# A two-layer mixer trunk on one core: the first dilated pair's probabilities turned by transposes and DMAs instead of on TensorE

## What is computed

```
s = einsum(q, gathered k) * scale; s = where(valid, s, -inf)   # for windows (128,1), (512,4), (2048,16)
p = softmax(concat of the three, axis=-1)
out = sum over the windows of einsum(p_c, gathered v_c)
y_d = dilated(dq, dk, d_v) * silu(g_d)
x = x + concat([y_a, y_b, y_c, y_d]) @ w_out
```

## Time and profile before

| what | value |
|---|---|
| median of 3 runs | 807.24 us (807.17 to 807.83) |
| the profiled execution's own time | 806.72 us |
| its span | 804.9 us |
| PE busy | 796.2 us (99%) |
| DVE, ACT, POOL busy | 608.1, 469.2, 127.5 us |
| TensorE clock granted, all 40 slices | 9 tenths or more |
| DMA engines busy, by slice | 4 to 9 tenths |
| PE's idle time by cause, all lines together | 5.0 us, of it 1.3 us before L921 |

### The profile page before, as it was taken

The page is one execution under the profiler, slowest core; times in us unless marked ns, Lnnn a source line. Parts: engine busy times, 40 slices in busy tenths (PEclk is TensorE's granted clock), DMA queues, the critical chain, the costliest instruction groups (busy, mean ns, idle before and its releaser), DMA issues.

```text
span 804.9 us, 10724 instructions
## 1 busy us (share of the span) xinstructions
PE 796.2 (99%) x3900; PEld 674.0 (84%) x3900; DVE 608.1 (76%) x1066; ACT 469.2 (58%) x762; POOL 127.5 (16%) x199
## 2 busy tenths in 40 slices
PE   8999999999999999999999999999999999999998
PEld 5888888999887888888888888889998888888886
DVE  6678889787899776665764967988779987865552
ACT  6666543857955676443556465447777566664431
POOL 7100000020432421102100000002105242211000
PEclk9999999999999999999999999999999999999999
DMA  8966534575698987869866655365767988968563
GB/s 332 344 219 215 182 132 152 160 252 187 211 283 262 288 256 243 261 208 280 259 213 187 194 152 196 111 188 170 228 200 238 268 277 256 274 196 286 187 195 115
DMA packets 54117, 178.22 MB, mean 221 GB/s; under 512 B 7408, under 2 KB 8352, under 8 KB 54064
## 3 DMA queue, kind: packets, MB, share of 16 engines
q1 hardware_dynamic: 44736, 149.98, 57.2%
q0 software_dynamic: 9008, 27.34, 12.3%
q10 hardware_dynamic: 320, 0.21, 0.1%
HBM read 161.76 MB, written 15.75 MB: 221 GB/s over the span
## 4 chain that ended last, share of the span: by engine, by line
PE 78%; DVE 12%; issue 3%; ACT 3%; DMA 3%; POOL 0%; SPq 0%; DVEq 0%; ACTq 0%; POOLq 0%
PE gemm L764 24%; PE gemm L755 24%; PE gemm L756 23%; DVE w_lo L1434 4%; DVE arena L1395 3%; DMA raw<-in_weights_dram 1%; DMA arena<-dil_q_squares 1%; PE pairs L921 1%; ACT w_hi L1051 1%; DVE u L1694 1%; PE pairs L811 1%; DVE arena L1523 1%; ACT arena L1231 1%; DMA mla_P_squares<-u 1%; PE pairs L946 0%
## 5 line engine op out<-in xcount | busy, mean ns | idle before, releaser
L1434 DVE TENSOR_TENSOR w_lo<-raw,w_hi 128x1024 fp32r<-128x1024 f32 (+2 forms) x279 | 322.1, 1163 | 151.8 <-ACT w_hi L1051 150.7
L755 PE MATMUL gemm<-w_hi,a_hi 128*128 128x512 f32 (+2 forms) x1080 | 414.5, 384 | 0.7 <-ACT w_hi L1051 0.7
L756 PE MATMUL gemm<-w_hi,a_lo 128*128 128x512 f32 (+2 forms) x1080 | 408.9, 379 | 0.0
L1051 ACT ACTIVATE w_hi<-raw 128x1024 fp32r<-128x1024 f32 (+2 forms) x279 | 278.2, 1011 | 212.7 <-PE gemm L764 138.6
L764 PE MATMUL gemm<-w_lo,a_hi 128*128 128x512 f32 (+2 forms) x1080 | 278.2, 379 | 0.3
L755 PEld LDWEIGHTS gemm<-w_hi,a_hi 128*128 128x128 f32 x1080 | 202.9, 188 | 37.3 <-issue 1.7
L756 PEld LDWEIGHTS gemm<-w_hi,a_lo 128*128 128x128 f32 x1080 | 202.9, 188 | 33.5
L764 PEld LDWEIGHTS gemm<-w_lo,a_hi 128*128 128x128 f32 x1080 | 199.5, 188 | 36.4 <-DVE w_lo L1434 1.9
L637 POOL TENSOR_TENSOR st<-st,powers 128x4 f32<-128x4 f32 (+2 forms) x8 | 3.7, 461 | 296.6 <-ACT arena L1129 213.0
L1081 ACT ACTIVATE u<-gemm,st 128x512 f32<-128x512 f32 (+2 forms) x36 | 21.3, 644 | 14.6 <-PE gemm L764 14.6
L1395 DVE STREAM_TRANSPOSE arena<-u 32x256 f32<-32x256 f32 x64 | 27.9, 436 | 1.2
(11 more groups left out here) (218 smaller groups left out, 672.8 us busy)
## 6 DMA issues: line engine op xcount, KB each, us to landing
raw<-in_weights_dram SPq DMA_DIRECT2D x225, 512.0 KB, 4.3
raw<-in_weights_dram SPq DMA_DIRECT2D x38, 384.0 KB, 3.6
raw<-in_weights_dram SPq DMA_DIRECT2D x16, 344.0 KB, 3.3
y_squares<-arena POOLq DMA_DIRECT2D x8, 512.0 KB, 3.4
arena<-y_squares POOLq DMA_DIRECT2D x32, 128.0 KB, 5.5
x<-in_x_dram SPq DMA_DIRECT2D x4, 512.0 KB, 6.2
o<-ssd_rows SPq DMA_DIRECT2D x8, 256.0 KB, 5.3
param_rows<-in_params_dram SPq DMA_DIRECT2D x2, 904.0 KB, 6.6
```

The source lines that it names most:

```text
L755: pe.matmul(acc_t[t], a_hi[:, k, tok[t]], hi, start=k == 0, stop=False)
L756: pe.matmul(acc_t[t], a_lo[:, k, tok[t]], hi, start=False, stop=False)
L1051: A_(w_hi[:, g % SPLIT, 0:c], raw[:, g % RAW, 0:c], ACT.Copy).then_inc(hi_done, 1)
L1434: TT(w_lo[:, g % SPLIT, 0:c], raw[:, g % RAW, 0:c], w_hi[:, g % SPLIT, 0:c].bitcast(F32), ALU.subtract).then_inc(split_done, 1)
```

## The change

The probabilities of the first dilated pair go by squares too. Six PE transposes per layer (`dil PT 0`) fall away with their PSUM pair; DVE gets two stream transposes (`dil P 0 squares`, slot 102, directly behind the taps); POOL gets one DMA out and four back; ACT's `dil PT 0` now copies from `u` in place of PSUM, at slot 107. The tile that is written and read back is the one that mla P 0 used, in `u`. The second pair stays on PE. On PE `dil O 0` moves from slot 104 to 106, `dil PT 1` from 106 to 107, `dil O 1` from 108 to 109. DVE's scores of pair 1 wait for the new squares where they waited for the PE transposes. POOL's order at the end of a layer becomes dil P 0, y 0, y 1, y 2, and dil P 0's way out takes over the place behind the wait for mla P 1.

```diff
-          "dil PT 0": 102, "dil S 1": 103, "dil O 0": 104, "dil PT 1": 106, "dil O 1": 108}
+          "dil S 1": 103, "dil O 0": 106, "dil PT 1": 107, "dil O 1": 109}
...
-LAST_READER |= {f"dil PT {_i}": ("act", f"dil PT {_i}") for _i in range(2)}
+LAST_READER["dil PT 1"] = "act", "dil PT 1"
...
+        SQUARES["dil P 0"] = SQUARES["mla P 0"]
...
-                for name in ("y 1", "y 0", "y 2"):
+                for name in ("dil P 0", "y 0", "y 1", "y 2"):
                     squares_out(l, name)
                     squares_back(l, name)
...
-                    if m == "mla":
-                        act_.wait_ge(squares_in[f"mla P {i}"], 16 * 4 * (l + 1))
-                        if i:
-                            act_.wait_ge(*pe("mla O 0"))
+                    if (m, i) != ("dil", 1):
+                        act_.wait_ge(squares_in[f"{m} P {i}"], 16 * 4 * (l + 1))
+                        if (m, i) != ("mla", 0):
+                            act_.wait_ge(*pe("mla O 0" if i else "mla O 1"))
...
-                                if n == (slot(f"dil PT {i}") if m == "dil" else slot(f"mla O {i}", 1)):
+                                if n == (slot("dil PT 1") if (m, i) == ("dil", 1) else slot(f"{m} O {i}", 1)):
                                     probs_T(m, i)
...
                     if m == "dil":
-                        v.wait_ge(*(pe("dil PT 0") if i else me("mla P 1 squares")))
+                        v.wait_ge(*me("dil P 0 squares" if i else "mla P 1 squares"))
...
                                     if m == "dil":
                                         taps(i)
+                                        if not i:
+                                            probs_squares("dil", 0)
```

More of the change, by code:

```diff
@@ L250 @@
         "mla cT, ssd Y, mla rT, "
-        "mla S 0, mla S 1, mla O 0, dil S 0, mla O 1, dil PT 0, dil S 1, dil O 0, "
+        "mla S 0, mla S 1, mla O 0, dil S 0, mla O 1, dil S 1, dil O 0, "
         "dil PT 1, dil O 1",
     "act":
-        "x rs sum, evac 0, evac 1, gla lr, gla abs, gla exp, gla ln, evac 2, gla E 0, gla E 1, "
-        "gla E 2, gla cross, gla E 3, gla E 4, evac 3, gla E 5, gla E 6, gla E 7, evac 4, ssd abs, ssd exp, "
-        "ssd eA, ssd ln, conv 3 1, gla rs sum, conv 3 0, evac 5, ssd silu 1, "
@@ L257 @@
-        "mla crs sum, ssd gcol, ssd silu 0, evac 6, ssd exp 0, mla cT, ssd xD, ssd exp 1, mla q 0, evac 7, mla q 1, mla rs 0 sum, "
[3 rows of a table removed]
-    "dve":
[L262 to L268, removed]
[3 rows of a table removed]
+        "x rs sum, evac 0, evac 1, gla lr, gla abs, gla exp, gla ln, evac 2, gla E 0, gla E 1, gla E 2, gla cross, gla E 3, "
@@ new lines @@
+        "gla E 4, evac 3, gla E 5, gla E 6, gla E 7, evac 4, ssd abs, ssd exp, ssd eA, ssd ln, conv 3 1, gla rs sum, conv 3 0, "
+        "evac 5, ssd silu 1, mla crs sum, ssd gcol, ssd silu 0, evac 6, ssd exp 0, mla cT, ssd xD, ssd exp 1, mla q 0, evac 7, "
+        "mla q 1, mla rs 0 sum, mla kv 0, mla kv 1, mla rs 1 sum, dil rs 0 sum, evac 8, dil rs 1 sum, mla qT, evac 9, mla rT, "
+        "mla P 0, ssd rs sum, mla P 1, evac 10, mla PT 0, dil q, dil P 0, mla PT 1, evac 11, dil P 1, dil PT 0, yT 0, dil PT 1, "
@@ new lines @@
+        "yT 1, yT 2, evac 12, yT 3",
+    "dve":
+        "pad, gla turn, gla dots, gla zero 0, gla zero 1, gla la, gla scan 0, gla scan 1, gla D 0, gla D 1, gla W 0, gla D 2, "
+        "gla W 1, gla D 3, gla W 2, gla merge 1, gla D 4, gla W 3, gla merge 2, gla D 5, gla W 4, gla merge 3, gla D 6, gla W 5, "
+        "gla merge 4, gla D 7, gla W 6, gla merge 5, gla W 7, gla merge 6, ssd turn, gla merge 7, ssd dt0, ssd dt, ssd la, "
+        "conv 1 0, conv 1 1, gla o, conv 1 2, conv 1 3, conv 1 4, conv 1 5, ssd row, conv 0 0, conv 0 1, conv 0 2, conv 0 3, "
+        "conv 0 4, conv 0 5, ssd CB, mla cn, ssd x squares, ssd E 0, mla cT, ssd E 1, ssd M 0, ssd xdt, ssd M 1, mla n 0 0, "
+        "mla n 0 1, ssd yT, mla q squares, mla n 1 0, ssd y squares, mla n 1 1, mla rope products, mla rope, mla k squares, "
+        "dil n 0 0, dil n 0 1, dil n 1 0, dil n 1 1, dil rope 0 products, dil rope 0, dil rope 1 products, dil rope 1, gated 1, "
+        "mla max 0, mla nmax 0, dil q squares, dil k squares, mla P 0 squares, mla max 1, mla nmax 1, y 1, mla P 1 squares, "
[3 rows of a table added]
@@ L1264, in probs_T @@
                 def probs_T(m, i):
-                    if m == "mla":
-                        act_.wait_ge(squares_in[f"mla P {i}"], 16 * 4 * (l + 1))
-                        if i:
-                            act_.wait_ge(*pe("mla O 0"))
-                        to, squares = PT.rearrange("p r (c i a) -> p i (r c) a", i=4, a=32), SQUARES[f"mla P {i}"][1].rearrange("p (i x a) -> p i x a", i=4, a=32)
-                        A_(to, squares, ACT.Copy).then_inc(*signal("act", f"mla PT {i}"))
+                    if (m, i) != ("dil", 1):
+                        act_.wait_ge(squares_in[f"{m} P {i}"], 16 * 4 * (l + 1))
+                        if (m, i) != ("mla", 0):
+                            act_.wait_ge(*pe("mla O 0" if i else "mla O 1"))
+                        to, squares = PT.rearrange("p r (c i a) -> p i (r c) a", i=4, a=32), SQUARES[f"{m} P {i}"][1].rearrange("p (i x a) -> p i x a", i=4, a=32)
+                        A_(to, squares, ACT.Copy).then_inc(*signal("act", f"{m} PT {i}"))
                         return
@@ L1741, in taps, with probs_squares @@
                     last.then_inc(*sig(f"dil P {i}"))
-                def probs_squares(i):
-                    v.wait_ge(*act(f"mla P {i}"))
-                    if not i:
+                def probs_squares(m, i):
+                    v.wait_ge(*(act if m == "mla" else me)(f"{m} P {i}"))
+                    if (m, i) == ("mla", 0):
                         v.wait_ge(*me("dil k squares"))
-                    to = SQUARES[f"mla P {i}"][0].rearrange("p (f r c a) -> p r f c a", f=4, r=2, c=3)
+                    to = SQUARES[f"{m} P {i}"][0].rearrange("p (f r c a) -> p r f c a", f=4, r=2, c=3)
                     for r in range(2):
                         last = v.transpose(to[:, r], Pb[:, r].rearrange("p (c f b) -> p f c b", c=3, f=4))
-                    last.then_inc(*sig(f"mla P {i} squares"))
+                    last.then_inc(*sig(f"{m} P {i} squares"))
                 def out_heads(m, i):
@@ L1900, in _ @@
                             if n == SQUARES[f"mla P {i}"][2]:
-                                probs_squares(i)
+                                probs_squares("mla", i)
                         for j in Y_TURN:
```

## The result

The changed kernel takes 824.3 us (median of 4 runs, 823.2 to 827.4) where the kernel before takes 807.2: a ratio of 1.0214, 95% interval 1.0189 to 1.0238. Slower, as forecast, but by 17 us instead of 7.6, and beyond the upper end of the range, 820.0. The profiled execution took 823.24 us, its span 821.3: 16.4 more than before.

The account below looks back on a forecast made before the run. PE, busy 796.2 of 804.9 us, was taken to set the time. Removed transposes -1.36 and stalls +2.4 and +6.6 gave +7.6 us, so 814.8 us forecast, range 808.0 to 820.0.

Parts of the forecast that it names:

- The mechanism: POOL's extra trip lands y 2 late; behind yT 2 on ACT, evac 12 and hi make PE stall at slot 115.
- What is added on POOL: One more round trip ahead of y 0, y 1, y 2 in POOL's serial queue; yT 2 5.2 and 9.0 us late.
- The moves of O 0, PT 1 and O 1 on PE by one or two slots change no sum: PE's moved jobs around slots 104 to 109 were costed at nothing.
- The bounds: Extra trip costs the chain 5.8 to 10.4 us, second layer 5.7 to 12.1; total +2.0 to +13.0, 809.2 to 820.2 us.
- The argument that ACT's wait frees the engines: ACT waiting at yT 1 pauses SP's weight loads, so y 2's out was taken as 6.1 us, 7.0 in second layer.
- The sum: -1.36 us for transposes removed, +2.4 and +6.6 us for PE's stalls at slot 115: +7.6 us.
- What is removed: Six PE transposes per layer, 0.68 us each block, 1.36 us for both layers, all gained on PE.
- The new copy is late: Rival: PE waits at dil O 0 for dil P 0's copy, 0.2 us or 2 us more per layer; 815 to 818; chance 0.03.
- Every leg contended, 820 us: Rival: all POOL legs run at contended prices, giving the upper bound, 820 us; chance 0.06.
- The gain alone: Rival: every POOL leg takes its free price, no stall, PE keeps the 1.36 us; 805.9 us; chance 0.17.

Follow-up runs that it names:

- run 3: Kernel before plus DVE's squares and an unread round trip of dil P 0, placed last, behind y 2 on POOL; 806.87 us, ratio 0.998.
- run 4: Changed kernel with only POOL's order altered: each way out issued ahead of the way back before it; 807.3 us, ratio 0.9993.
- run 9: Changed kernel with POOL issuing y 1's and y 0's outs before its wait for mla P 1's squares, then dil P 0's out, then backs; 807.95 us, ratio 0.9993.
- Run 8: Changed kernel with evac 12 put ahead of yT 2 on ACT; 810.87 us, ratio 1.0029.
- run 7: Changed kernel with y 1 ahead of y 0 on POOL, behind dil P 0; 822.41 us, ratio 1.0149.
- run 10: Kernel before plus two unread round trips of dil P 0, one after the other, ahead of y 1, y 0, y 2; no slot moved; 831.27 us, ratio 1.0282.
- run 2: Kernel before plus DVE's squares and one unread round trip of dil P 0 ahead of y 1, y 0, y 2; 811.39 us, ratio 1.0043.
- run 1: Kernel before with only the changed kernel's moved slots and orders; all transposes on PE, no extra trip; 808.22 us, ratio 0.999.
- run 5: Changed kernel, unedited, on a second chip; 823.07 us, ratio 1.0168 to the kernel before there.
- run 6: Kernel before with the moved slots and an unread round trip ahead of y 0, y 1, y 2; PE keeps its transposes; 820.5 us, ratio 1.0116.
- run 11: Changed kernel with the early outs of run 9 and evac 12 ahead of yT 2 on ACT; 807.2 us, ratio 0.9986.

## Why the prediction was right in its mechanism and wrong in its size

**The mechanism held.** Runs 3, 4 and 9 leave all the work in place and only move it in POOL's queue: the loss disappears. Run 8 leaves y 2 late and takes evac 12 out of the way: most of it disappears. So in the changed kernel the serial chain, the late y 2, and evac 12 and hi behind yT 2 are the cause, in the order in which the prediction has them. (Runs 7 and 10 have a loss of the same kind by another result: there y 0 is late, and ACT's wait at yT 0 is what PE pays.) The rows that it named are there: four trips on POOL, L1070 waiting for `y_squares`, the first load of slot 115 released by ACT's w_hi, PE with 12 matmuls fewer. Their sizes are not: ACT waits 6.4 and 4.2 us at yT 2 where 5 and 9 were named, 6.1 and 8.5 at yT 1 where 4 was, 4.2 and 5.0 at yT 0 where nothing was, and PE is busy for longer, not shorter.

The forecast sum was +7.6 and the spans differ by 16.4. The 8.8 between them are three terms: the stalls 12.74 for 9.0 (+3.7), the clock 3.99 for nothing (+4.0), the gain -0.33 for -1.36 (+1.0).

**"What is added on POOL", the value for y 1's out: the step that failed.** It was taken as 4.6 and 4.8 us, "the place that y 2's out had". Measured 7.63 and 7.73. That row was read as if a leg's price belonged to its place in time. It belongs to what else runs beside it, and the change had altered that. In the kernels whose slots are not moved the out issued at 301 to 304 us, and its fellow in the second layer, takes what the prediction says: 3.7 and 4.8 (before), 4.9 and 4.2 (run 2), 5.3 and 4.5 (run 3). With the moved slots it takes 6.4 and 8.8 (run 1, with no trip at all), 7.6 and 7.7 (after), 7.5 and 7.6 (run 5), 7.7 and 6.8 (run 6), 8.4 and 8.0 (run 7, so the order of y 0 and y 1 isn't it), 6.8 and 8.0 (run 8). The sentence "The moves of O 0, PT 1 and O 1 on PE by one or two slots change no sum" is right for PE's own work and wrong for this leg. What differs is the traffic: in the row that was read the loads paused. The DMA queues while y 2's out was pending before, and while y 1's was in the changed kernel, first layer (packets, MB, share):

```profile
q0 software_dynamic: 231, 0.73, 66.9%
q1 hardware_dynamic: 68, 0.28, 28.9%
```

```profile
q0 software_dynamic: 312, 0.96, 45.0%
q1 hardware_dynamic: 327, 1.22, 44.9%
```

0.28 MB of weights (q1) in 3.66 us against 1.22 in 7.63. The legs behind a back line up by it: 3.76 us with no weights at all in run 7, 3.92 and 3.79 in run 10; 4.81 with 0.72 MB (before, second layer); 6.4 with 1.12 (run 1); 7.63 and 7.73 with 1.22 and 1.42 (after). Others do not fit: y 2's outs in run 2, 5.58 with 0.05 MB and 8.82 with 0.43, and in after, 7.67 and 9.71 with 1.05 each. A long leg also gives the loads more time, so the amounts prove no rate; but the legs near 3.8 stand behind a back and are hardly longer than the 3.6 of an out in a free queue, so standing there costs little by itself.

By step, first layer: the new out 0.8 us later than taken, its leg 4.0 for 3.6, y 0's 6.75 for 7.9, y 1's 7.63 for 4.6, y 2's 7.67 for 6.1. Together y 2's back is 4.5 us later than forecast (318.3 for 313.8), its landing somewhat faster, and the stall 5.8 for 2.4. Second layer: 5.0 for 3.6, 6.7 for 9.4, 7.7 for 4.8, 9.7 for 7.0, that is 3.8 later, but y 2 was at ACT 4.7 us after its back was issued, where 7.85 were taken. The stalls, 6.9 for 6.6, agree only because two errors cancel, and 2.0 of them lie ahead of slot 115, at a hi and a lo that yT 1's wait of 8.5 us had delayed; the prediction had no wait there.

The bounds failed with the same step. They added one trip of 5.8 to 10.4 us to a chain whose other legs stayed as they were, so that yT 2 would be at most 7.5 us late in the first layer; it was 9.0 late. In the second it was 9.8 late, within its 5.7 to 12.1.

**The argument that ACT's wait frees the engines** was right and put in the wrong place. The prediction used it for y 2's leg alone. It was not strong enough there: ACT waited 6 us at yT 1, and 1.05 MB of weights moved all the same. Where ACT waits 14 and 13 us, as in run 7, y 2's out does drop to 3.8 in both layers; where it waits 9, as in run 2, it takes 5.6 and 8.8. In the changed kernel y 0 comes first, yT 0 waits only 4.2 and 5.0 us, and the loads go on.

The Trainium skill, DMA: Bandwidth & Descriptors, "Anatomy of one DMA — SWDGE (gpsimd) path", gives by its 2.0 us and 436 GB/s an estimate of 3.2 us for such a leg; the legs with the loads paused, 3.76 to 3.92, come near it, the 6.4 to 9.7 under loads don't.

**"The sum": no term for the clock.** Every price was taken at the full rate. This step failed too, as a term put at nothing. A stall that is forecast at 6.6 us should have raised the question what PE does after it. It is 1.9 + 2.1 us here, and without it the time would have been 820.3, at the edge of the range.

**"What is removed"** was right as a price: 0.69 in run 9's second layer. In the changed kernel a wait of 0.37 for the MLA's copy in the first layer and 0.8 us lost ahead of slot 102 in the second took most of it back. Neither is shown to come from the change: run 3's trace has such a wait for the MLA's copy, 0.3 us, too, and the scatter ahead of slot 102 is in every kernel.

**The rivals.** "The new copy is late" did not come in the changed kernel (0.2 us was forecast, the trace has none), but it does in other traces with the new copy: 0.8 us in run 9, 1.4 in run 8, 2.6 in run 11, each in one layer. "Every leg contended, 820 us" was nearest for the first layer; it had been held against the pause of the loads, with 6 in 100. "The gain alone" is what runs 4 and 9 are: the mechanism works where no trip waits for another, and even then 1.36 us is less than the runs can tell.

## What to carry to other kernels

Before putting a transfer at the head of an in-order queue, ask who is last in it and what stands behind that one's reader: the 2.4 to 2.8 us of room in each layer were worth more than the 1.4 us of work that was saved, and issuing the outs ahead of the backs keeps them. A transfer's duration read from a trace holds only with the traffic that ran beside it; check the other queues' bytes in that window before it is moved to another one, and ask whether the change itself moves that traffic, as the moved slots did here. When a forecast contains a stall of PE of several microseconds, add the unit behind it at the lower clock.

## What was not expected of the hardware

**The clock after a wait.** PE's waits in this stretch and the granted clock behind them: 1.7 and 2.6 us (runs 8 and 2), clock 1.00; 3.8, 4.5, 4.6, 4.8, 5.4, 5.9, 6.5, 7.8 and 11.8 us (runs 6, after, 5, 7 and 10), clock 0.50 when PE went on. The level is 1.2 GHz instead of 2.4, and until PE is back at its pace it costs 1.3 to 2.5 us: 1.9 and 2.1 in after, 2.5 and 1.4 in run 5, 2.3 in run 6, 1.3 and 2.3 in run 7, and 1.8 twice in run 10, after the two longest waits. So it doesn't grow with the wait. The Trainium skill, TensorE: Matmul & The Clock Gate, "Part 1: The HAM clock gate (the "warmup" mystery)", says that an idle TensorE falls back to the lower of its two levels and that the first work after it runs there. The trace agrees, by the windows of after and of run 10 above.

**Loads and round trips hold each other back.** When y is late for long enough, ACT stops, the loads stop, and the late transfer speeds up (3.8 us instead of 7 to 8 in run 7, 3.9 and 3.8 in run 10). So delays do not simply add along the chain. Run 2's second layer, 8.8 us with few weights beside it, shows that this is not the whole rule; and whether run 2 was cheap by ACT's early stop or by its unmoved slots is not separated by these runs.

**Open.** That the loads run on in the stretch from 300 us with the slots moved, and pause there before, is read from the traces; which of the moved jobs on PE, ACT and DVE does it was not tested. PE's busy time grew by 5.7 us, of which 4.0 less 1.4 are named here; ends of matmuls are modelled in that number, and the rest was not followed.
